# Weight panels of 512 columns by half the rows, for three norms, the queries and the keys

## The chip, the cores and the metric

The kernel runs on one core of a Trainium2 chip. The metric is the device time of one execution, in microseconds (us). The kernel before was run three times: median 2101.73 us, from 2101.66 to 2103.25. A further execution was recorded by the profiler.

## What is computed

Two networks run one after the other over 256 latent tokens `x` and 256 context tokens `ctx` of width 1024, all in float32. The first is two layers of a transformer block. Each layer modulates a normalised input, projects it, and mixes it with two attentions and an MLP:

```python
h_c = modulate(rms_norm(x_ctx, g_attn[l]), csh1, csc1)
h = modulate(rms_norm(x_lat, g_attn[l]), sh1, sc1)
gl, mq, mk, mv, nq, nk, nv = mixer_proj(h, *proj_w)      # h @ w_in, then the low-rank q and kv
...
x_lat = x_lat + gt1 * gated_merge(gl, y_mla, y_na, w_mla_o[l], w_na_o[l], w_out[l])
h2 = modulate(rms_norm(x_lat, g_mlp[l]), sh2, sc2)
x_lat = x_lat + gt2 * squared_relu_mlp(h2, w_ff1[l], w_ff2[l])
```

The context takes the same path in layer 0, and in layer 1 gives only keys and values. The second network starts from this `x_lat` and its own `ctx_2`: an mLSTM layer and then an attention layer whose queries, keys, values and gate are `h @ w_in` of width 2560. Only the latent tokens are returned.

## The kernel before

**Data.** The activations stand transposed in SBUF: `xT` holds 8 chunks of 128 rows for 512 tokens (columns 0 to 255 context, 256 to 511 latent). A norm writes its result as two float32r arrays, `XAh` (rounded) and `XAl` (what rounding left). Weights are treated likewise. They come as **panels** of 1 MB: 8 chunks of 128 rows (`nk`) by 256 columns. The SP queue brings panels in the order of the list that `plan` (line 140) makes, into three `raw` buffers in turn; panel i is fetched when the low half of panel i-3 is made. ACT copies a panel to `whi` (line 1142, `hi`) and DVE subtracts that from the raw panel to give `wlo` (line 1716, `lo`), each in two halves of 1024 columns. There are two `whi`/`wlo` buffers, so the copy of panel i+1 has to wait until PE has used panel i-1 (`p.before`). Of six panels in `POOL_PANELS` (line 117) the low part is made by POOL (line 2366).

**Products.** Each product is three matmuls, high by high, high by low and low by high. `weight_left` (555) has the weights stationary and 512 tokens moving (256 where only latents count): lines 567 to 569. `tokens_left` (594) has 128 tokens stationary and 256 weight columns moving: lines 604 to 606; it makes the na queries and keys, the low-rank queries, the values, and the last queries. It runs through the 8 chunks of one panel for one tile of 128 tokens, with a bank of PSUM for each tile and panel. PSUM banks are taken in turn from six.

**Order.** Each engine's program is written out by hand and runs in that order; they meet at semaphores only. In ACT and DVE a call `begin(p)` makes the split of the panel that follows p. So where ACT or DVE wait, everything behind waits too.

**Norms.** A norm is a sum of squares over the 8 chunks, one matmul with ones on PE (`rms`, 655), a root on ACT (1189) and a reciprocal on DVE (1766), and then chunk by chunk: DVE scales (`scaled`, L1711), ACT writes `XAh` (L1200) and, for odd chunks, the shifted value (L1202), and then DVE (even chunks) or POOL (odd chunks, L2381) writes `XAl`. The context half goes first, the latent half after. PE meets the norm with `weight_pair` (572, lines 588 to 590), and before the last attention layer with its own loop (1060 to 1062): both run over the context half and then the latent half of 8 chunks, and wait before each chunk until its `XAl` is there. `weight_pair` issues 6 matmuls of 256 columns a chunk and half: one panel. The second panel follows as a whole with `weight_left`.

**Three norms** matter here: `n1.0` at the start (at 40 us), `n2.0` ahead of layer 0's MLP (at 492 us), and `s1` ahead of the last attention layer (at 1932 us). Before `n2.0` and `s1` the last residual panel is multiplied by halves while the norm starts (`turn`: 657 on PE, 1204 on ACT, 1791 on DVE).

**The last attention layer** (1043, 1608, 2271) has two panels of keys and values (`atkv`, 256 columns each), four of queries (`atq`, latent tokens only: two tiles), four of the gate (`atz`), then transposes and softmax. ACT takes keys out (L1231), squares them (L1616), DVE sums and normalises them (L2293, L1817, L1702), rotates keys and queries (L1702), and in between makes the low parts of the query panels.

## Time and profile before

| | |
|---|---|
| median of three runs | 2101.73 us |
| the profiled execution, its own time | 2103.66 us |
| its span | 2101.9 us |
| PE busy (matmuls) | 2036.6 us, 97%, 13298 instructions |
| DVE busy | 1133.3 us, 54% |
| ACT busy | 906.8 us, 43% |
| POOL busy | 75.2 us, 4% |
| data moved by DMA | 277.20 MB, mean 132 GB/s |

The profiled execution took 1.8 us longer than its span, which is what lies around the first and last instruction. A matmul's duration in the profile includes a modelled end that overlaps the next one, so "97% busy" doesn't tell how much of the time PE worked at its pace: the distance between the starts of two matmuls does. `LDWEIGHTS` (PEld) overlaps the matmuls.

### The profile page before, as it was taken

Reading aid. Unit: us, or ns where it says so; the run is one execution under the profiler, and the core shown is the slowest. Engines: PE = TensorE matmul, PEld = TensorE weight load, DVE = VectorE, ACT = ScalarE, POOL = GpSimd, SP = SyncE. Lnnn points to the kernel's source line nnn. Section 1 sums busy time; section 2 is a strip of 40 time slices with the busy share of each in tenths; the row PEclk is TensorE's granted clock in tenths of the full one; section 3 lists DMA queues with packets and bytes.
Section 4 is the critical chain, followed back from the end, with each engine's and each line's share of the span. In section 5 each row is a group of like instructions: output and inputs, shape, how many; then the busy total and the mean of one; then the engine's idle time right before and its main releaser. Section 6 shows DMA issues by size and latency. Waiting matters only on the chain. (4 is left out here: it accounts for less than half of the span.)

```text
span 2101.9 us, 32389 instructions
## 1 busy us (share of the span) xinstructions
PE 2036.6 (97%) x13298; PEld 1708.4 (81%) x13298; DVE 1133.3 (54%) x2224; ACT 906.8 (43%) x1648; POOL 75.2 (4%) x89
## 2 busy tenths in 40 slices
PE   5999999999999999999999999999999999999998
PEld 3898767778777777799789899987877777887977
DVE  4447662446433343567665776632555454445876
ACT  4436762325323131355664555433343332234565
POOL 1000000002000000100000000010000000001000
PEclk8999999999999999999999999999999999999999
DMA  7222015533344444433117554444211243222311
GB/s 291 105 77 94 32 42 194 196 132 119 140 182 190 169 161 180 189 134 114 50 63 260 201 185 177 183 165 160 101 61 41 81 180 140 97 85 81 132 50 41
DMA packets 47107, 277.20 MB, mean 132 GB/s; under 512 B 4464, under 2 KB 12784, under 8 KB 16752
## 3 DMA queue, kind: packets, MB, share of 16 engines
q1 hardware_dynamic: 42080, 266.94, 33.7%
q10 hardware_dynamic: 4736, 7.34, 1.0%
q8 instruction: 106, 1.74, 0.3%
q0 software_dynamic: 144, 0.85, 0.1%
q14 instruction: 41, 0.34, 0.0%
HBM read 273.01 MB, written 2.10 MB: 131 GB/s over the span
## 5 line engine op out<-in xcount | busy, mean ns | idle before, releaser
L567 PE MATMUL ps<-t 128*128 128x512 f32 (+1 forms) x2232 | 776.1, 348 | 6.1 <-DVE t L1716 4.6
L568 PE MATMUL ps<-t 128*128 128x512 f32 (+1 forms) x2232 | 768.9, 344 | 0.0
L569 PE MATMUL ps<-t 128*128 128x512 f32 (+1 forms) x2232 | 768.8, 344 | 0.0
L1716 DVE TENSOR_TENSOR t<-t 128x1024 fp32r<-128x1024 f32 (+2 forms) x366 | 410.2, 1162 | 246.0 <-ACT t L1142 245.2
L567 PEld LDWEIGHTS ps<-t 128*128 128x128 f32 x2232 | 421.4, 189 | 72.8 <-issue 9.0
L569 PEld LDWEIGHTS ps<-t 128*128 128x128 f32 x2232 | 421.3, 189 | 52.7
L568 PEld LDWEIGHTS ps<-t 128*128 128x128 f32 x2232 | 421.4, 189 | 51.8 <-issue 0.7
L1142 ACT ACTIVATE t<-t 128x1024 fp32r<-128x1024 f32 (+2 forms) x378 | 359.1, 999 | 189.1 <-PE ps L569 155.4
L1702 DVE TENSOR_TENSOR t<-t 128x512 f32<-128x512 f32 (+10 forms) x621 | 239.6, 405 | 218.7 <-ACT t L1231 78.9
L1231 ACT ACTIVATE t<-ps 128x256 f32<-128x256 f32 (+3 forms) x270 | 121.6, 468 | 402.0 <-PE ps L569 260.5
L604 PE MATMUL ps<-t 128*128 128x256 f32 (+1 forms) x812 | 239.8, 295 | 0.7 <-DVE t L1716 0.5
L606 PE MATMUL ps<-t 128*128 128x256 f32 (+1 forms) x812 | 232.9, 287 | 0.0
L605 PE MATMUL ps<-t 128*128 128x256 f32 (+1 forms) x812 | 232.9, 287 | 0.0
L1711 DVE SCALAR_TENSOR_TENSOR t<-ps,t 128x256 f32<-128x256 f32 (+2 forms) x176 | 83.1, 496 | 179.5 <-PE ps L569 161.8
L604 PEld LDWEIGHTS ps<-t 128*128 128x128 f32 x812 | 155.1, 191 | 9.1 <-issue 3.0
L605 PEld LDWEIGHTS ps<-t 128*128 128x128 f32 x812 | 155.2, 191 | 3.6 <-issue 2.2
L606 PEld LDWEIGHTS ps<-t 128*128 128x128 f32 x812 | 155.1, 191 | 1.4
L1711 DVE SCALAR_TENSOR_TENSOR t<-t 128x256 f32<-128x256 f32 (+6 forms) x226 | 97.5, 457 | 48.5 <-ACT t L1231 34.0
L1702 DVE TENSOR_TENSOR t<-ps,t 128x128 fp32r<-128x128 f32 (+5 forms) x134 | 52.1, 393 | 86.5 <-ACT t L1594 35.2
L634 PE MATMUL ps<-t 128*32 128x256 f32 x1152 | 74.9, 399 | 18.8 <-DMA t<-in_panels 18.1
L1254 ACT ACTIVATE t<-ps,t 128x512 f32<-128x512 f32 (+1 forms) x128 | 87.0, 696 | 10.9 <-DVE t L1702 10.9
L1179 ACT ACTIVATE t<-t 128x256 f32<-128x256 f32 (+1 forms) x62 | 30.9, 503 | 122.8 <-DVE t L1711 106.9
(151 smaller groups left out, 1749.2 us busy)
## 6 DMA issues: line engine op xcount, KB each, us to landing
t<-in_panels SPq DMA_DIRECT2D x236, 1024.0 KB, 4.9
t<-in_panels SPq DMA_DIRECT2D x19, 512.0 KB, 3.8
t<-in_panels SPq DMA_DIRECT2D x6, 768.0 KB, 4.1
t<-in_window ACTq DMA_DIRECT2D x4, 768.0 KB, 4.2
t<-in_ctxT SPq DMA_DIRECT2D x1, 1024.0 KB, 13.3
t<-in_xT SPq DMA_DIRECT2D x1, 1024.0 KB, 15.5
t<-in_ctxT ACTq DMA_DIRECT2D x1, 1024.0 KB, 5.6
t<-in_xT ACTq DMA_DIRECT2D x1, 1024.0 KB, 9.5
```

Source lines behind the costliest of these rows:

```text
L567: e.matmul(o, hi[:, k, w], xh[:, c0:c1], start=k == 0, stop=False)
L568: e.matmul(o, hi[:, k, w], xl[:, c0:c1], start=False, stop=False)
L569: t = e.matmul(o, lo[:, k, w], xh[:, c0:c1], start=False, stop=k == p.nk - 1)
L604: e.matmul(o, xh[:, r], hi[:, k, n0:n1], start=k == 0, stop=False)
L605: e.matmul(o, xh[:, r], lo[:, k, n0:n1], start=False, stop=False)
L606: t = e.matmul(o, xl[:, r], hi[:, k, n0:n1], start=False, stop=k == p.nk - 1)
L1142: e.activation(p.half(whi[p.buf], a), p.half(raw[p.slot], a), ACT.Copy).then_inc(*up(se, ("hi", p.i, a)))
L1231: e.activation(o, i, func, scale=scale).then_inc(*up(se, ("read", key), *names))
L1254: e.activation(work[:, 2 * par + g, x * w:x * w + w], banks(("s", s, i, g))[:, x * w:x * w + w], ACT.Exp, scale=sc_, bias=nm[:, c:c + 1], ...
L1702: e.tensor_tensor(o, a, b, op).then_inc(*up(ve, *names))
L1711: e.scalar_tensor_tensor(o, a, s_, b, o1, o2).then_inc(*up(ve, *names))
L1716: e.tensor_tensor(p.half(wlo[p.buf], a), p.half(raw[p.slot], a), p.half(whi[p.buf], a).bitcast(F32), ALU.subtract).then_inc(*up(ve, ("lo", ...
```

## The change

Eighteen of the panels keep their 1 MB but hold 4 chunks of 128 rows by 512 columns: half the rows and twice the columns. Two such panels replace two of 8 chunks by 256 columns. These are the na queries and keys of both layers (8 panels), the last queries (4), the last keys and values (2), and the first two panels behind each of the norms `n1.0` (`cq`) and `n2.0` (`ff1`) (4). The rest of the list is unchanged. The core of the diff:

```diff
-POOL_PANELS = [("uq", 0, 0), ("ff1", 0, 0), ("ckv", 1, 0), ("uq", 1, 0), ("mq", 0), ("atkv", 0)]
+POOL_PANELS = [("uq", 0, 0), ("ckv", 1, 0), ("uq", 1, 0), ("mq", 0), ("atkv", 0)]
...
+    def halves(key, w, n0, first=0):
+        for a in range(2):
+            panel((*key, first + a), w, 4 * a, 4, n0, 512)
...
+            def weight_four(keys, pair, xs, s, amid=None):
+                o = [bank(key) for key in keys]
+                for x in "cl":
+                    a, b, _ = PARTS[x]
+                    for k in range(8):
+                        p = pair[k // 4]
...
+                        if x == "c" and k % 4 == 0:
+                            weights(p)
+                        rest(p, k % 4)
+                        if amid and x == "c" and k == amid[0]:
+                            amid[1]()
+                        e.wait_ge(*done(("xlo", s, k, x)))
+                        for j in range(4):
+                            w = slice(j * 128, j * 128 + 128)
+                            e.matmul(o[j][:, a:b], hi[:, k % 4, w], xh[:, a:b], start=k == 0, stop=False)
+                            e.matmul(o[j][:, a:b], hi[:, k % 4, w], xl[:, a:b], start=False, stop=False)
+                            t = e.matmul(o[j][:, a:b], lo[:, k % 4, w], xh[:, a:b], start=False, stop=k == 7)
...
+                        if x == "l" and k == 3:
+                            t.then_inc(*up(pe, ("used", p.i)))
+
+            def tokens_half(key, p, xs, tile, last):
+                k0 = p.src[2]
+                o = banks(key) if k0 else bank(key)
...
+                for k in range(4):
+                    xh, xl = xs(k0 + k)
+                    rest(p, k)
+                    e.matmul(o, xh[:, r], hi[:, k, :], start=k0 + k == 0, stop=False)
+                    e.matmul(o, xh[:, r], lo[:, k, :], start=False, stop=False)
+                    t = e.matmul(o, xl[:, r], hi[:, k, :], start=False, stop=k0 + k == 7)
...
                     for tile in tiles if n == "q" else range(4):
-                        tokens_left(("na", l, n, a, tile), p, 0, 256, xa, tile)
+                        tokens_half(("na", l, n, tile), p, xa, tile, tile == 3)
...
                     for k in range(8):
                         shifted(s, k, "c", kind, l, vb)
...
+                        if p2 and k in (3, 5):
+                            hi(p2, (k // 4,))
                         if k == 5:
                             rms(s, "l")
-                    begin(p)
+                    if p2:
+                        nxt[0] = p2.i + 1
+                    else:
+                        begin(p)
...
-                                                       (lambda: last(1, "l"), lambda: stat(s, 7, "l"))])
+                                                       (lambda: last(1, "l"), lambda: stat(s, 7, "l")),
+                                                       *[(lambda a=a: lo(pair, a), lambda: None) for a in range(2) if pair]])
```

`weight_four` (the norms `n1.0` and `n2.0`) issues 12 matmuls of 256 columns a chunk and half, for four chunks of output in four banks, and holds two panels at once: the first is given back after chunk 3 of the latent half, the second at the end. The loop before the last attention layer does the same with tokens stationary: per chunk and half 6 matmuls of 512 columns. `tokens_half` runs 4 chunks of 512 columns for each tile and keeps the tile's bank open until the second panel; results are taken out only then, 512 columns at a time. Columns times matmuls stay the same everywhere; the program has 432 matmuls fewer (528 fewer in the tokens-left products, 96 more where the second panel of `cq` and `ff1` had run with 512 tokens moving).

ACT's and DVE's part: the high and low halves of the second panel of each pair are now made within the context half of the norm, before chunks 4 and 6. In `n1.0` all four halves of the first two panels lie there (before chunks 0, 2, 4 and 6). The low part of `ff1`'s first panel moves from POOL to DVE.

**Place 1: ACT, context half of the norm before the last attention layer.** Names: `t_24` is `xT`, `t_25` is `XAh`, `t_43` is `work`, `t_27` to `t_29` are the raw panels, `t_30` and `t_31` the two `whi`, `t_39` the modulation, `ps_121` PSUM, `t_42` the root. Before, from chunk 2 on:

```order
L1200 ACTIVATE t_25<-t_43,t_39 128x256 x2
L1202 ACTIVATE t_43<-t_43,t_39 128x256
L1179 ACTIVATE t_43<-t_24 128x256
L1200 ACTIVATE t_25<-t_43,t_39 128x256 x2
L1202 ACTIVATE t_43<-t_43,t_39 128x256
L1189 ACTIVATE t_42<-ps_121,t_21 128x256
L1200 ACTIVATE t_25<-t_43,t_39 128x256 x2
L1202 ACTIVATE t_43<-t_43,t_39 128x256
L1142 ACTIVATE t_30<-t_29 128x1024 x2
```

After, from the same point (L1213 is the line that was L1142, L1271 was L1200, L1273 was L1202, L1260 was L1189):

```order
L1271 ACTIVATE t_25<-t_43,t_39 128x256 x2
L1273 ACTIVATE t_43<-t_43,t_39 128x256
L1250 ACTIVATE t_43<-t_24 128x256
L1213 ACTIVATE t_30<-t_29 128x1024
L1271 ACTIVATE t_25<-t_43,t_39 128x256 x2
L1273 ACTIVATE t_43<-t_43,t_39 128x256
L1213 ACTIVATE t_30<-t_29 128x1024
L1260 ACTIVATE t_42<-ps_121,t_21 128x256
L1271 ACTIVATE t_25<-t_43,t_39 128x256 x2
L1273 ACTIVATE t_43<-t_43,t_39 128x256
```

The copy of the second key/value panel came behind the eight context chunks in one piece; now its halves stand before chunk 4 and before the latent half's root.

**Place 2: DVE, start of the norm ahead of the MLP.** `t_32` and `t_33` are the two `wlo`, `t_36` the modulation. Before, from the last whole sum of squares on (L1711 with `ps_121` is a residual):

```order
L1702 TENSOR_TENSOR t_43<-t_43 128x512
L1702 TENSOR_TENSOR t_36<-ps_121,t_19 128x16
L1711 SCALAR_TENSOR_TENSOR t_36<-t_36,t_19 128x16
L1711 SCALAR_TENSOR_TENSOR t_24<-ps_121,t_36,t_24 128x256
L1702 TENSOR_TENSOR t_43<-t_43 128x256
L1711 SCALAR_TENSOR_TENSOR t_24<-ps_121,t_36,t_24 128x256
L1702 TENSOR_TENSOR t_43<-t_43 128x256
L1766 RECIPROCAL t_42<-t_42 128x256
```

After (L1788 was L1716, L1774 was L1702, L1783 was L1711, L1838 was L1766):

```order
L1774 TENSOR_TENSOR t_43<-t_43 128x512
L1788 TENSOR_TENSOR t_33<-t_28,t_31 128x1024 x2
L1774 TENSOR_TENSOR t_36<-ps_121,t_19 128x16
L1783 SCALAR_TENSOR_TENSOR t_36<-t_36,t_19 128x16
L1783 SCALAR_TENSOR_TENSOR t_24<-ps_121,t_36,t_24 128x256
L1774 TENSOR_TENSOR t_43<-t_43 128x256
L1783 SCALAR_TENSOR_TENSOR t_24<-ps_121,t_36,t_24 128x256
L1774 TENSOR_TENSOR t_43<-t_43 128x256
L1838 RECIPROCAL t_42<-t_42 128x256
```

The low part of `ff1`'s first panel, which POOL made, stands on DVE ahead of the residuals of the last two chunks and the reciprocal.

**Place 3: ACT, last attention layer, behind the taking out of the keys.** `t_106` holds the keys, `t_105` the values, `t_110` the keys' sums, `t_102` the queries. Before:

```order
L1616 ACTIVATE t_43<-t_106 128x256 x4
L1142 ACTIVATE t_31<-t_27 128x1024 x2
L1620 ACTIVATE t_110<-t_110 128x16
L1231 ACTIVATE t_105<-ps_121 128x256 x4
L1142 ACTIVATE t_30<-t_28 128x1024 x2
L1231 ACTIVATE t_102<-ps_121 128x256 x2
L1142 ACTIVATE t_31<-t_29 128x1024 x2
```

After, from the last tile on (L1687 takes out keys, L1688 values):

```order
L1687 ACTIVATE t_106<-ps_121 128x256
L1688 ACTIVATE t_105<-ps_121 128x256
L1692 ACTIVATE t_43<-t_106 128x256 x4
L1695 ACTIVATE t_110<-t_110 128x16
L1213 ACTIVATE t_30<-t_28 128x1024 x2
L1213 ACTIVATE t_31<-t_29 128x1024 x2
L1308 ACTIVATE t_102<-ps_121 128x512 x2
```

Before, the copy of a query panel stood between the squares (L1616) and the root (L1620), and another behind the values. Now keys and values are taken out together, and both copies (of the second and third query panel) stand behind the root, which waits for DVE's sums.

## Rows read from the trace of the kernel before

**Rows 1.** Groups by line and shape, PE, whole span: busy, mean ns, idle before.
```profile
L588 PE MATMUL ps<-t 128*128 128x256 f32 x144 | 45.8, 318 | 17.6 <-DVE t L1711 13.3 <-POOL t L2381 4.3
...
L1060 PE MATMUL ps<-t 128*128 128x256 f32 x64 | 19.0, 297 | 5.4 <-DVE t L1711 3.1 <-DVE t L1716 1.3 <-POOL t L2381 1.0
```

**Rows 2.** Page, costliest groups: halves of the weight splits, on DVE and ACT.
```profile
L1716 DVE TENSOR_TENSOR t<-t 128x1024 fp32r<-128x1024 f32 (+2 forms) x366 | 410.2, 1162 | 246.0 <-ACT t L1142 245.2
...
L1142 ACT ACTIVATE t<-t 128x1024 fp32r<-128x1024 f32 (+2 forms) x378 | 359.1, 999 | 189.1 <-PE ps L569 155.4
```

**Rows 3.** Timeline, PE, queries of layer 0: start us, us, engine line op out<-in.
```profile
97.10 0.28 PE L605 MATMUL ps<-t 128*128 128x256 f32 x1
...
99.98 0.28 PE L605 MATMUL ps<-t 128*128 128x256 f32 x1
```

**Rows 4.** Timeline, PE, 512-column matmuls over XAh and XAl.
```profile
90.17 0.39 PE L569 MATMUL ps<-t 128*128 128x512 f32 x1
...
93.57 0.39 PE L569 MATMUL ps<-t 128*128 128x512 f32 x1
```

**Rows 5.** Timeline, PE, tokens-left matmuls of 512 weight columns (ukv).
```profile
175.20 0.40 PE L604 MATMUL ps<-t 128*128 128x512 f32 x1
...
175.90 0.39 PE L604 MATMUL ps<-t 128*128 128x512 f32 x1
```

**Rows 6.** Timeline, PE, first norm: first matmul, clock's rise, third panel's first.
```profile
40.06 0.55 PE L588 MATMUL ps<-t 128*128 128x256 f32 x1 [6.15 <-DVE t L1711]
...
43.27 0.39 PE L588 MATMUL ps<-t 128*128 128x256 f32 x1 [0.31 <-DVE t L1711]
...
67.28 0.39 PE L567 MATMUL ps<-t 128*128 128x512 f32 x1
```

**Rows 7.** Timeline, DVE, same norm, context half.
```profile
38.30 1.23 DVE L1716 TENSOR_TENSOR t<-t 128x1024 fp32r<-128x1024 f32 x1 [3.05 <-ACT t L1142]
...
41.11 1.21 DVE L1716 TENSOR_TENSOR t<-t 128x1024 fp32r<-128x1024 f32 x1
...
45.65 3.16 DVE L1711 SCALAR_TENSOR_TENSOR t<-t 128x256 fp32r<-128x256 f32 x6 [0.18 <-ACT t L1200]
```

**Rows 8.** Timeline, PE, norm ahead of the MLP: first matmul, third panel's first.
```profile
492.16 0.39 PE L588 MATMUL ps<-t 128*128 128x256 f32 x1
...
519.52 0.39 PE L567 MATMUL ps<-t 128*128 128x512 f32 x1
```

**Rows 9.** Timeline, same norm's start on POOL, DVE and ACT.
```profile
480.37 4.93 POOL L2366 TENSOR_TENSOR t<-t 128x1024 fp32r<-128x1024 f32 x2 [343.85 <-ACT t L1142]
...
481.82 1.23 DVE L1702 TENSOR_TENSOR t<-t 128x256 f32<-128x256 f32 x1 [0.54 <-ACT t L1179]
...
484.71 1.28 ACT L1187 ACT_TABLE_LOAD   x1
```

**Rows 10.** Timeline, PE, attention: norm's first, latent half, queries, gate 2.
```profile
1932.42 0.35 PE L1060 MATMUL ps<-t 128*128 128x256 f32 x1 [0.43 <-DVE t L1711]
...
1942.85 0.36 PE L1060 MATMUL ps<-t 128*128 128x256 f32 x1 [1.29 <-DVE t L1711]
...
1962.78 0.28 PE L604 MATMUL ps<-t 128*128 128x256 f32 x1
...
2000.03 0.39 PE L567 MATMUL ps<-t 128*128 128x256 f32 x1
```

**Rows 11.** Timeline, DVE, attention layer, up to the rotation of the queries.
```profile
1955.03 1.39 DVE L2293 TENSOR_REDUCE t<-t 128x4 f32<-128x256 f32 x4
...
1957.83 1.64 DVE L1702 TENSOR_TENSOR t<-t 128x16 f32<-128x16 f32 x5
...
1964.34 2.36 DVE L1716 TENSOR_TENSOR t<-t 128x1024 fp32r<-128x1024 f32 x2 [4.88 <-ACT t L1142]
...
1972.45 2.35 DVE L1716 TENSOR_TENSOR t<-t 128x1024 fp32r<-128x1024 f32 x2
...
1981.62 2.23 DVE L1702 TENSOR_TENSOR t<-t 128x256 f32<-128x256 f32 x6
```

158 lines of the change are left out of this document (93 added, 65 removed).

## The prediction

> **What bounds the kernel now.** I read the groups by line first, then the distance between matmul starts, then the timeline at each stretch that the change touches. PE works almost without a gap, so the time is PE's pace times its matmuls, plus the few places where it waits. The groups name those: line 588 idled 17.6 us before its matmuls over five norms, nearly all of it for `XAl` from DVE (13.3) and POOL (4.3), and line 1060, the last attention layer's norm, 5.4 us [rows 1]. Two of those five norms (`n1.0`, `n2.0`) and the attention's change here. The pace: from 97.10 to 99.98 lie 24 matmuls of 256 columns, 0.120 us each [rows 3]; from 90.17 to 93.57 fifteen of 512 columns, 0.2267 us each [rows 4]. So two narrow ones (0.240) cost 0.0133 us more than one wide one: each matmul carries a fixed part. But wide isn't always that fast: in the `ukv` product, the only one before with tokens stationary and 512 weight columns moving, three take 0.70 us, 0.2333 each [rows 5].
>
> **Term 1, narrow to wide in the na queries and keys.** Layer 0 had 4 tiles x 4 panels x 24 = 384 matmuls, layer 1 2 tiles x 2 panels x 24 + 4 x 2 x 24 = 288. They become half as many: 192 + 144 = 336 pairs. At 0.0133 us a pair: 2.6 us + 1.9 us = **4.5 us**. Bounds: at `ukv`'s pace [rows 5] a pair saves 0.0067, in all 2.2 us; if a wide one took two narrow ones' time, nothing. I take 4.5, since both operands there are `XAh`/`XAl` and `whi`/`wlo`, the same arrays as in rows 4 with their roles changed, while `ukv` has another stationary array. What follows (low-rank queries, rotations, transposes) starts when these products are taken out, so it moves with them. The fewer, wider takings-out lie beside PE.
>
> The Trainium skill ("TensorE: Matmul & The Clock Gate", back-to-back issue gap) gives the gap as N/2.4 + 2.5 ns, so an estimate by it is 109.2 ns and 215.8 ns and a pair would save 2.5 ns, 0.8 us here instead of 4.5. Rows 3 and 4 show 120 and 226.7 ns, and I go by them.
>
> **Term 2, the first norm.** Before, PE ran from its first matmul at 40.06 to the third panel's first at 67.28: 27.2 us [rows 6], for 96 x 0.120 + 48 x 0.2267 = 22.4 us of work. The norm is the reason: a pair of context chunks with half a split in it takes DVE 41.11 - 38.30 = 2.8 us, and a pair without 3.16 / 2 = 1.6 us [rows 7], against PE's 12 x 0.12 = 1.44 us for a pair. After, PE has 24 matmuls for a pair, 2.9 us. All four context pairs now carry half a split (2.8 each, 11.2 in all, against 11.5 of work) and the latent ones none (1.6 against 2.9). PE should run without a stall to the end: 192 x 0.12 = 23.0 us. To this comes the low clock: until 43.27 the matmuls ran at 1.2 GHz (twelve of them in 3.2 us) [rows 6]; now PE has fifteen to put into that time, and 3.2 us at half speed lose some 1.4 us. 24.5 against 27.2: **2.7 us**. Bounds: nothing, if the pairs with a split starve PE, to 3.5. Line 567's 48 wide matmuls have become 96 narrow ones here and in term 3; that costs 48 x 0.0133 = 0.6 us each time and is inside these sums.
>
> **Term 3, the norm ahead of the MLP.** 492.16 to 519.52, 27.4 us [rows 8]. After: 23.0 plus 0.35 for the matmul with ones, plus what follows. DVE now makes the low part of `ff1`'s first panel itself, 2 x 1.16 = 2.3 us [rows 2], ahead of the last two residuals. It is not all late: DVE had waited there for PE's products, and POOL's 4.9 us of work ran beside [rows 9] and is gone. A sum of squares of 256 columns took 1.23 us under it [rows 9], and six like operations later took 2.23, 0.37 each [rows 11]. I get the last sum 0.2 us later and, with the 1.28 us table load behind it on ACT [rows 9], the reciprocal 0.6 us later. PE is busy with modulation rows until 492.1 and doesn't see that, but for 0.2 us. The two halves of the second panel fall into pairs 3 and 4, for which PE has 2.9 us each. So 23.8 against 27.4: **3.6 us**. Behind it, four chunks of output are full at once (two before), at some 2 us each on ACT and DVE: 8 us, and then the next split (2 us and 1.2 us), 11.2 us; PE has 10.9 us in the third panel, but its first outputs are full 1.1 us ahead of the end. It just fits. Bounds 0 and 4.
>
> The Trainium skill ("GPSIMD Engine Reference", specifications and key points) says that GpSimd shares its SBUF interfaces with VectorE, with contention for DVE instructions with two SBUF inputs; the 1.23 us beside POOL and 0.37 us without agree. Without that relief the reciprocal would be some 1.6 us late, and the sum 1 us smaller.
>
> **Term 4, the last attention layer.** PE began the norm at 1932.42, its latent half at 1942.85 after a wait of 1.29 us, and the queries at 1962.78 [rows 10]. Its work in that stretch is 192 narrow matmuls, 23.0 us, of 30.4 us. After: 96 wide ones, 8 chunks x 6 x 0.2267 = 10.9 us a half. The context half is bound by the norm: from 10.4 us it grows by the two halves on DVE, 2.3 us, less about 0.4 of slack, to 12.4. The latent half starts at 1944.85 and ends at 1955.75, **7.0 us earlier**. Not all is kept, since DVE is the next bound. The keys can be squared only when both key and value banks are full and taken out, about 1957.9. DVE's sums then end at 1958.4 instead of 1956.4 (1955.03 + 1.39), and the normalised keys at 1961.5 instead of 1959.5 (1957.83 + 1.64) [rows 11]. Behind it comes the second query panel's low half: ready 1962.7, where PE, after 24 wide matmuls (5.44 us), wants it at 1961.2: 1.5 us of stall. It ends at 1963.85 instead of 1966.70 (1964.34 + 2.36), the rotations of the keys take 5.75 us (to 1972.45) as before, and the third panel's low half is there at 1969.6 + 1.2 = 1970.8, where PE wants it at 1962.8 + 5.4 = 1968.2: another 2.6 us. From there DVE's chain stays 4 us ahead of before, and PE's start of gate 2 moves from 2000.03 [rows 10] to some 1995.9: **4.1 us**. The softmax behind it is unchanged. Bounds: 0, if DVE's chain keeps its old times, and 8.3 (7.0 and 96 pairs of the queries at 0.0133).
>
> **Sum.** 4.5 + 2.7 + 3.6 + 4.1 = 14.9 us. The profiled execution took 2103.66 us (span 2101.9 and 1.8 around it) and would take 2088.8. The median of the runs is 1.9 us below it: 2101.73 - 14.9 = **2086.8 us**. DMA moves the same panels, and each slot is given back earlier or at the same point of the program; I price it at nothing.
>
> **Rivals.**
>
> A. *The wide matmuls aren't faster.* They run at `ukv`'s 0.2333 us, or the fixed part is smaller than rows 3 and 4 say. For it: rows 5 is the only example of this form. Against: another stationary array there. Term 1 falls to 2.2 and term 4 by 0.5 or so: 12.1 us, 2089.6 us; with no gain at all, 2091.9. Chance 0.17. The Trainium skill's gap ("TensorE: Matmul & The Clock Gate", back-to-back issue gap) gives an estimate of 2090.5 us.
>
> B. *The attention layer keeps nothing.* DVE's chain of keys and queries (or the query split behind the root on ACT) is what gate 2 waits for, at its old time. For it: DVE goes from a split at 1964.34 over one at 1972.45 to rotations at 1981.62 [rows 11] with little between. Against: each link that I followed starts earlier. 10.8 us, 2090.9 us. Chance 0.13.
>
> C. *It keeps everything*, because the keys' chain is shorter than I think: 7.0 to 8.3 in term 4, and 4.0 and 3.5 in terms 3 and 2: 20 us, 2081.7 us. Chance 0.09.
>
> D. *Slower: the next split becomes the bound of every wide panel.* A pair holds both `whi` buffers and `tokens_half` needs each panel whole sooner. ACT waits in order for a buffer and for full banks, so if a panel's copy (2.0 us) and low half (1.2 us) can begin only when PE is through with the one before, each of the 12 panels of queries and keys costs up to 3.2 us: 38 us, less 14.9, 2125 us. It decides from 1.6 us a panel (19 us). Against: a token panel is used up as before in four tiles, and its other buffer is free meanwhile; only in layer 1's and the last queries is PE's time for a panel as short as 5.4 us, and it was 5.8 before. Chance 0.03.
>
> E. *Two or three of these partly, nothing left to measure*: within 0.2% (4.2 us, about what a measurement of this kernel can tell from no change). Chance 0.04.
>
> **How the numbers follow.** Forecast 0.54, its own range 2084.5 to 2089. The range to cover 8 in 10 reaches to C on one side (2081.5) and past A and B on the other (2092.5, where terms 1 and 4 both halve and the norms give 5.5); D, E and worse sums lie outside. Faster by over 0.2%: forecast, A, B, C, 0.93. Same 0.04, slower 0.03.
>
> **What would show it.** Wide matmuls over the weights 0.227 us apart in the na stretch (A: 0.233 or more). No gap over 0.3 us in PE between 43 us and the third panel at about 64.5; in the MLP's norm the third panel 23.8 us after the first matmul. In the attention layer a latent half that starts 12.4 us after the context half, queries 23.3 us after it, then two waits of PE for low halves (line 1788 of the changed kernel), of 1.5 and 2.6 us, at the second and third query panel. POOL without its 4.9 us ahead of the MLP. Wrong would be: PE waiting at na panels (D), or gate 2 no closer to the norm's start than the 67.6 us of before (B).

## The result, and the profile after

The changed kernel took 2089.43 us (median of 4 runs, 2088.06 to 2092.04), the kernel before 2101.69 us in the 4 runs beside it (2100.68 to 2103.25). The ratio is 0.9943, its 95% interval 0.9925 to 0.996: 12 us faster, where 14.9 were forecast (2086.8 us; the range of 2081.5 to 2092.5 holds the result, which lies just above the forecast's own range of 2084.5 to 2089). The profiled execution took 2092.04 us, with a span of 2089.3, against 2103.66 and 2101.9 before: 11.6 us by its time, 12.6 by its span. One execution of a kernel further down, the one that takes the gate early, took 3346.17 us at a mean granted clock of 0.56; the ratios leave it out.

Three rows of the groups by shape (line, engine, operation, names, shapes, count | busy us, mean ns | idle us before, by what ended it), changed kernel. They answer to [rows 1]:

```profile
L640 PE MATMUL ps<-t 128*128 128x512 f32 x144 | 57.4, 399 | 3.7 <-DVE t L1788 3.7
L622 PE MATMUL ps<-t 128*128 128x256 f32 x128 | 37.3, 292 | 4.0 <-DVE t L1783 4.0
...
L1128 PE MATMUL ps<-t 128*128 128x512 f32 x32 | 12.9, 403 | 1.0 <-DVE t L1783 1.0
```

Line 588's 17.6 us of idle time came from five norms. The two that changed had 10.8 of them, 8.0 at the first (6.15 of these ahead of its first matmul) and 2.8 at the MLP's. Now line 622 (these two, with four chunks) has 4.0, all ahead of its very first matmul. The three norms that keep the old form, line 598 of the changed kernel, still wait 7.6 us. Line 1060's 5.4 us have become 1.0 in line 1128 (the attention layer's keys and values). What is new is the first row: the wide token products wait 3.7 us, all for line 1788, the low half of a weight panel. PE is busy 97% of the span. The rest of the reading goes by places. Timeline of PE in the changed kernel (start us, busy us, engine, line), the first norm and the na queries:

```profile
41.06 0.55 PE L622 MATMUL ps<-t 128*128 128x256 f32 x1 [4.01 <-DVE t L1783]
...
65.58 0.40 PE L577 MATMUL ps<-t 128*128 128x512 f32 x1
...
94.55 0.47 PE L640 MATMUL ps<-t 128*128 128x512 f32 x1
...
98.76 0.39 PE L640 MATMUL ps<-t 128*128 128x512 f32 x1
...
104.65 0.39 PE L642 MATMUL ps<-t 128*128 128x512 f32 x1
...
289.12 0.50 PE L577 MATMUL ps<-t 128*128 128x512 f32 x1
```

From the first norm's first matmul to its third panel 24.52 us (27.2 in [rows 6]). The wide matmuls over the weights stand 0.2265 us apart (26 of them from 98.76 to 104.65), the pace of [rows 4], not that of [rows 5]. From the first of the na queries (94.55) to the first product behind that layer's attention (289.12): 194.57 us. Then the MLP's norm, where the matmul with ones (line 709) waits for the last residual, and the last attention layer: norm, latent half, queries, second and third query panel, gates, softmax.

```profile
482.15 0.67 PE L709 MATMUL ps<-t 128*128 128x256 f32 x2 [0.86 <-DVE t L1774]
...
488.53 0.39 PE L622 MATMUL ps<-t 128*128 128x256 f32 x1
...
512.08 0.40 PE L577 MATMUL ps<-t 128*128 128x512 f32 x1
...
1922.77 0.47 PE L1128 MATMUL ps<-t 128*128 128x512 f32 x1 [0.44 <-DVE t L1783]
...
1935.74 0.47 PE L1128 MATMUL ps<-t 128*128 128x512 f32 x1 [0.33 <-DVE t L1783]
...
1946.74 0.39 PE L640 MATMUL ps<-t 128*128 128x512 f32 x1
...
1953.71 0.50 PE L640 MATMUL ps<-t 128*128 128x512 f32 x1 [1.37 <-DVE t L1788]
...
1961.81 0.50 PE L640 MATMUL ps<-t 128*128 128x512 f32 x1 [2.32 <-DVE t L1788]
...
1963.09 0.63 PE L641 MATMUL ps<-t 128*128 128x512 f32 x1
1963.52 0.63 PE L642 MATMUL ps<-t 128*128 128x512 f32 x1
...
1988.31 0.39 PE L577 MATMUL ps<-t 128*128 128x256 f32 x1
...
1996.22 0.70 PE L738 MATMUL ps<-t 64*128 64x512 f32 x2
```

The MLP's norm takes 23.55 us (27.4 in [rows 8]). In the attention layer both forecast waits are there, 1.37 and 2.32 us, at the second and third query panel. What follows the second was not forecast: the matmuls start 0.43 us apart, not 0.2267. The window says why (from:to, length, busy us of PE, PEld, DVE, ACT and POOL with the number of instructions, then PEclk, the granted clock as a share of full speed, and at the end the DMA engines' share and GB/s):

```profile
1961.80:1966.00 4.20, 4.19 (x11) 3.31 (x12) 3.71 (x10) 1.62 (x3) 0.00 (x0) 0.59 0.45 138
```

From 1962.5 on PE ran for 3.4 us at 1.2 GHz, and then at 2.4 again (PEclk 1.00 from 1966 on). What the drop costs, and whether it belongs to the wait, the runs have to tell.

Cut at the first matmul of each stage, the 12.5 us between the two first profiles come from these stretches:

| stretch | before | after | difference | forecast |
|---|---|---|---|---|
| start to first norm | 40.06 | 41.06 | +1.0 | 0 |
| first norm to na queries | 56.13 | 53.49 | -2.6 | -2.7 |
| na queries of layer 0 to the end of its attention | 197.04 | 194.57 | -2.5 | -2.6 |
| from there to the MLP's norm | 198.93 | 199.41 | +0.5 | 0.2, inside the next line's |
| MLP's norm to layer 1's na queries | 434.78 | 431.00 | -3.8 | -3.6 |
| layer 1's na queries and attention | 85.01 | 83.47 | -1.5 | -1.9 |
| from there to the last attention layer's norm | 920.47 | 919.77 | -0.7 | 0 |
| that norm to its softmax | 76.32 | 73.45 | -2.9 | -4.1 |
| softmax to the last matmul | 89.53 | 89.54 | 0.0 | 0 |

The 0.7 us in the third line from the end aren't part of the forecast: PE waits there once for a low half before (0.69 us, at 1120.45) and not after. The three kernels below with one of the old parts take 920.4 to 920.6 us for that stretch, the others 919.7 to 920.0 with one exception (next section); why, wasn't followed.

### The profile page after: what moved, and what is told of

The parts are those of the page before. It is cut to its first block and busy times, and to the rows that moved or that the text cites. A ratio compares the mean times of both kernels' runs of the same rounds, so it can differ in the third digit from the quotient of the medians.

```text
span 2089.3 us, 31507 instructions
## 1 busy us (share of the span) xinstructions
PE 2028.2 (97%) x12866; PEld 1684.1 (81%) x12866; DVE 1128.6 (54%) x2226; ACT 905.4 (43%) x1630; POOL 68.2 (3%) x87
## 5 line engine op out<-in xcount | busy, mean ns | idle before, releaser
L577 PE MATMUL ps<-t 128*128 128x512 f32 (+1 forms) x2200 | 763.8, 347 | 6.5 <-DVE t L1788 4.6
L579 PE MATMUL ps<-t 128*128 128x512 f32 (+1 forms) x2200 | 756.4, 344 | 0.0
L578 PE MATMUL ps<-t 128*128 128x512 f32 (+1 forms) x2200 | 756.2, 344 | 0.0
L1788 DVE TENSOR_TENSOR t<-t 128x1024 fp32r<-128x1024 f32 (+2 forms) x368 | 411.9, 1160 | 260.9 <-ACT t L1213 260.1
L577 PEld LDWEIGHTS ps<-t 128*128 128x128 f32 x2200 | 415.4, 189 | 71.8 <-issue 9.4
L579 PEld LDWEIGHTS ps<-t 128*128 128x128 f32 x2200 | 415.3, 189 | 51.4
L578 PEld LDWEIGHTS ps<-t 128*128 128x128 f32 x2200 | 415.5, 189 | 50.7 <-issue 0.7
L1213 ACT ACTIVATE t<-t 128x1024 fp32r<-128x1024 f32 (+2 forms) x378 | 359.5, 999 | 207.1 <-PE ps L579 155.3
L1774 DVE TENSOR_TENSOR t<-t 128x512 f32<-128x512 f32 (+10 forms) x621 | 233.2, 395 | 206.5 <-ACT t L1308 73.2
L1308 ACT ACTIVATE t<-ps 128x512 f32<-128x512 f32 (+1 forms) x244 | 115.9, 493 | 368.5 <-PE ps L579 253.0
L1783 DVE SCALAR_TENSOR_TENSOR t<-ps,t 128x256 f32<-128x256 f32 (+2 forms) x176 | 83.1, 496 | 181.0 <-PE ps L579 160.9
L658 PE MATMUL ps<-t 128*128 128x256 f32 (+1 forms) x524 | 157.9, 301 | 0.4 <-DVE t L1788 0.2
L660 PE MATMUL ps<-t 128*128 128x256 f32 (+1 forms) x524 | 151.4, 289 | 0.0
L659 PE MATMUL ps<-t 128*128 128x256 f32 (+1 forms) x524 | 151.4, 289 | 0.0
L1783 DVE SCALAR_TENSOR_TENSOR t<-t 128x256 f32<-128x256 f32 (+6 forms) x226 | 99.5, 466 | 46.5 <-ACT t L1308 33.9
L658 PEld LDWEIGHTS ps<-t 128*128 128x128 f32 x524 | 99.7, 190 | 8.8 <-issue 3.0
L659 PEld LDWEIGHTS ps<-t 128*128 128x128 f32 x524 | 99.8, 190 | 3.7 <-issue 2.2
L660 PEld LDWEIGHTS ps<-t 128*128 128x128 f32 x524 | 99.7, 190 | 1.4
L1774 DVE TENSOR_TENSOR t<-ps,t 128x128 fp32r<-128x128 f32 (+5 forms) x134 | 52.1, 393 | 88.2 <-ACT t L1667 35.1
```

The lines of the kernel that those rows point to most:

```text
L577: e.matmul(o, hi[:, k, w], xh[:, c0:c1], start=k == 0, stop=False)
L578: e.matmul(o, hi[:, k, w], xl[:, c0:c1], start=False, stop=False)
L579: t = e.matmul(o, lo[:, k, w], xh[:, c0:c1], start=False, stop=k == p.nk - 1)
L658: e.matmul(o, xh[:, r], hi[:, k, n0:n1], start=k == 0, stop=False)
L659: e.matmul(o, xh[:, r], lo[:, k, n0:n1], start=False, stop=False)
L660: t = e.matmul(o, xl[:, r], hi[:, k, n0:n1], start=False, stop=k == p.nk - 1)
```

## The experiments

All kernels below were timed in five rounds against the kernel before on the same chip. Their ratios carry intervals of some 2.5 us to either side, so small differences are read from the stretches of the profiles, which repeat far better: in the profiles of three kernels with the same na stretch it took 194.59, 194.62 and 194.61 us. A difference "by the ratios" is that of two ratios times 2101 us.

### The changed kernel again, twice

Nothing is edited.

> The changed kernel once more, nothing altered: the yardstick for the kernels run beside it, 12 to 14 us under the kernel before. The question is the clock in the last attention layer. In the first profile of the changed kernel PE waited 2.32 us for the low half of the third query panel (line 1788), and the wide matmuls right behind that wait started 0.43 us apart from 1962.7 to 1966.0, at a granted clock of 0.59. If the wait brings the drop, it stands here again, at the same matmuls, and the queries' stretch is some 1.6 us longer than the matmuls and the two waits give. If it was chance in one execution, the matmuls behind the wait start 0.227 us apart here.

> The changed kernel again, as the yardstick for the three kernels run beside it: 12 to 14 us under the kernel before, with PE's two waits for low halves (line 1788) in the last attention layer, 1.4 and 2.3 us, and the low clock behind the second of them if it comes with the wait.

Measured: 2089.12 us, ratio 0.9943 (0.993 to 0.9955), and 2089.48 us, 0.9941 (0.9928 to 0.9953). The stretches repeat, but for four things. The first norm starts at 38.61 and 38.93 us in place of 41.06 (over all profiles of this study it lies between 36.1 and 42.2): the start varies more than most terms of the sum. Layer 1's stretch takes 81.76 and 81.83 us, not 83.47. The low clock behind the third query panel's wait is back in both, for 8 matmuls each. PE's first matmul behind that wait, in the first repetition, and then the window behind it:

```profile
1958.34 0.80 PE L640 MATMUL ps<-t 128*128 128x512 f32 x1 [2.35 <-DVE t L1788]
```

```profile
1958.20:1962.00 3.80, 3.66 (x9) 2.94 (x10) 3.37 (x9) 1.72 (x3) 0.00 (x0) 0.55 0.39 106
```

That matmul takes 0.80 us where the first profile's took 0.50: here the clock was down already when the wait ended. The fourth thing is a low clock with no wait at all. In the second repetition the stretch ahead of the last attention layer takes 921.8 us, and 1.5 of its extra 2 us lie here, in a row of narrow matmuls without an idle time of even 0.1 us in the 27 us before (the granted clock is 1.00 in the four us ahead and in the four behind):

```profile
1507.00:1511.00 4.00, 4.00 (x23) 4.00 (x22) 3.61 (x11) 0.27 (x1) 0.00 (x0) 0.58 0.00 0
```

The first repetition has 35 matmuls in the same window, at 1.00. So PE's clock can also fall where the kernel gives no reason.

### Narrow na panels again

The reading of the weights goes back to `cols(("na", l), w, 0, 8, 3104, 4128)`, and the products with it:

```diff
-                        tokens_half(("na", l, n, tile), p, xa, tile, tile == 3)
+                        tokens_left(("na", l, n, a, tile), p, 0, 256, xa, tile)
```

> The changed kernel with only the na queries and keys put back to matmuls of 256 columns (672 narrow ones in place of 336 wide ones). My theory: each pair of narrow ones costs 2 x 0.120 - 0.2267 = 0.0133 us more than a wide one, and PE is the bound all along: layer 0 2.6 us slower, layer 1 1.9 us slower, 4.5 us in all; the first trace of the changed kernel showed 2.4 and 1.5, so 3.9 at least. Rival A (a wide one saves half as much, or nothing): 2.2 us slower, or no difference. Rival D (the splits bind the wide panels): faster than the changed kernel.

Measured: 2091.05 us, ratio 0.996 (0.9947 to 0.9974), against 0.9943 for the changed kernel beside it: 3.6 us slower by the ratios. PE in this kernel, where the na stretch of layer 0 and that of layer 1 begin and end:

```profile
90.58 0.36 PE L657 MATMUL ps<-t 128*128 128x256 f32 x1
...
287.64 0.50 PE L576 MATMUL ps<-t 128*128 128x512 f32 x1
...
918.13 0.36 PE L657 MATMUL ps<-t 128*128 128x256 f32 x1
...
1001.49 0.68 PE L657 MATMUL ps<-t 128*128 128x256 f32 x1
```

Layer 0: 197.06 us against 194.59 in the changed kernel beside it, 2.47 us, so 2.47 / 192 = 0.0129 us for a pair. Layer 1: 83.36 against 81.76, 1.6 us, 0.0111 for a pair. Together 4.1 us. Rival A (half or nothing) and rival D (the splits bind) are out. Layer 1 also tells how the first two profiles are to be read: 85.01 before and 83.47 after are each some 1.65 us over these, and their difference is the same 1.5. In the changed kernel's first profile the granted clock shows it (0.78 and, in the four us ahead, 0.80, where the repetition has 1.00 at the same places):

```profile
998.20:1002.20 4.00, 4.00 (x27) 3.65 (x26) 2.93 (x7) 2.62 (x7) 0.00 (x0) 0.78 0.11 41
```

### The two norms in their old form

Both four-panel norms go back to two panels ahead and a third behind, and the low half of `ff1`'s first panel to POOL; the main piece of the edit:

```diff
-                        if kind == "cq" and not l and a < 2:
-                            if a == 0:
-                                weight_four([("cq", l, c) for c in range(4)], (p, at["cq", l, 1]), xa, s)
-                            else:
-                                used(p)
-                            wide = False
-                            continue
                         weights(p)
...
-                            weight_pair(keys, p, xa, parts, s)
+                            weight_pair(keys, p, xa, parts, s, None if last else (4, lambda: rms(s, "l")))
```

> The changed kernel with the two norms in four-panel form put back to two panels ahead and a third behind (the latent queries' first panels and ff1's first ones), with POOL's low half of ff1's first panel. My theory: the first norm's stretch to the third panel is 2.7 us longer again (27.2 in place of 24.5), the norm ahead of the MLP 3.8 us (27.4 in place of 23.6), less the 0.5 us by which the reciprocal came later in the changed kernel: 6.0 us slower. Rival: what the norms won is lost again behind them, where four chunks of output are full at once: then 3 us or less, and the third panels of the changed kernel show waits of PE that are not here.

Measured: 2094.09 us, ratio 0.9969 (0.9957 to 0.998), 5.5 us slower than the changed kernel by the ratios. From the first norm to the na queries:

```profile
41.77 0.55 PE L594 MATMUL ps<-t 128*128 128x256 f32 x1 [3.69 <-DVE t L1769]
...
97.91 0.47 PE L636 MATMUL ps<-t 128*128 128x512 f32 x1
```

56.14 us, as before the change (56.13). In the eleven profiles with the four-panel norm and nothing ahead of it that stretch takes 53.49 to 54.59 us, the median is 54.23. So the norm is worth 1.9 us, not the 2.6 of the first pair. The MLP's norm gives 3.9 us back (434.90 to layer 1's na queries against 431.00) and takes 0.45 (198.94 ahead of it against 199.39). 1.9 + 3.9 - 0.45 = 5.4, of 5.5 measured. The rival is out: nothing is lost behind the norms, and PE's third panels show no wait.

### The last attention layer in its old form

`atkv` and `atq` come as narrow panels again, with their loops; of the panels:

```diff
-    halves(("atkv",), w, 1024)
-    for i in range(2):
-        halves(("atq",), w, i * 512, 2 * i)
+    cols(("atkv",), w, 0, 8, 1024, 1536)
+    cols(("atq",), w, 0, 8, 0, 1024)
```

> The changed kernel with only the last attention layer's queries, keys and values (atkv, atq) put back to narrow panels. My theory after the first traces: this part of the change brought 2.4 us (gate 0 and gate 1 of that layer stood 2.3 and 2.1 us nearer to the norm's start), so 2.4 us slower. If the clock drop behind the third query panel's wait was chance and is usually absent, 4 us slower, as in term 4 of the prediction. Rival B (the layer keeps nothing, since DVE's chain of keys and queries is what the gates wait for): no difference.

Measured: 2090.33 us, ratio 0.9954 (0.9941 to 0.9966), 2.3 us slower by the ratios. Its norm and its softmax, and the softmax of the kernel before, whose norm is in [rows 10]:

```profile
1918.99 0.35 PE L1127 MATMUL ps<-t 128*128 128x256 f32 x1 [0.43 <-DVE t L1780]
...
1995.31 0.70 PE L737 MATMUL ps<-t 64*128 64x512 f32 x2 [0.88 <-ACT t L1304]
```

```profile
2008.74 0.70 PE L684 MATMUL ps<-t 64*128 64x512 f32 x2 [0.88 <-ACT t L1231]
```

76.32 us in both, against 73.45, 73.42 and 73.55 in the changed kernel: this part brings 2.9 us. Rival B is out, and so is the sum of 4.1. The expectation of 2.4 was read at gates 0 and 1 and left out what comes behind gate 2: from there to the softmax it is 8.7 us before and 7.9 in the changed kernel (1988.31 to 1996.22), where the first product of the softmax no longer waits 0.88 us for ACT. Why that wait is gone wasn't followed.

### The wait filled with work

Ten wide matmuls that nobody reads go on PE ahead of the third query panel; this is work beside what the reference asks for:

```diff
+                    if a == 2:
+                        o = bank(("filler",), (7,))
+                        for _ in range(10):
+                            t = e.matmul(o, XAh[:, 0, 0:128], XAh[:, 0, :], start=True, stop=True)
+                        t.then_inc(*up(pe, ("read", ("filler",))))
```

> The changed kernel with ten wide matmuls of no use (the tokens by themselves into a free bank, never read) put on PE ahead of the third query panel of the last attention layer, 2.27 us of work where PE waited 2.32 us for that panel's low half. My theory: the low clock behind the wait comes from the idle time; with the filler the wide matmuls of the third panel start 0.227 us apart at once, and this kernel is 1.6 us faster than the changed one, with the same work of use. Rival: the low clock there has nothing to do with the idle time (the power that the chip grants, or chance): the same time as the changed kernel, and the drop is still there or comes and goes in both.

Measured: 2087.73 us, ratio 0.9934 (0.9921 to 0.9946), 1.5 us faster than the changed kernel beside it by the ratios. The filler (line 1141), the third panel behind it, the norm's start and the softmax:

```profile
1921.06 0.47 PE L1128 MATMUL ps<-t 128*128 128x512 f32 x1 [0.44 <-DVE t L1788]
...
1957.59 2.43 PE L1141 MATMUL ps<-t 128*128 128x512 f32 x10
1960.12 0.50 PE L640 MATMUL ps<-t 128*128 128x512 f32 x1
1960.46 0.40 PE L641 MATMUL ps<-t 128*128 128x512 f32 x1
...
1992.98 0.70 PE L738 MATMUL ps<-t 64*128 64x512 f32 x2
```

The third panel starts 39.06 us behind the norm's start, as without the filler (1961.81 - 1922.77 = 39.04), and runs at 0.23 us from the start. The softmax comes 71.92 us behind the norm in place of 73.45: 1.5 us for doing more work. Seven profiles have that wait with nothing in it, and six of them show the drop; in the seventh, the kernel with narrow na panels, it is absent, and there too the softmax comes 71.91 us behind the norm. So the drop costs 1.5 us; it comes with the wait in six of seven profiles, and with the filler in neither of two (the second is below). That speaks for the wait as the cause, though two profiles are few. The 1.5 us by the ratios alone would lie within their intervals.

### A warm-up ahead of the first norm

Twenty matmuls of ones by ones, never read, where PE stands idle ahead of the first norm:

```diff
                 if not l:
                     rows_out()
+                    o = bank(("filler",), (7,))
+                    for _ in range(20):
+                        t = e.matmul(o[:, 0:128], ones[:, :], ones[:, :], start=True, stop=True)
+                    t.then_inc(*up(pe, ("read", ("filler",))))
```

> The changed kernel with twenty matmuls of ones by ones, 128 columns, never read, put on PE ahead of the first norm's first matmul, where PE stands idle for 3.6 to 4.8 us. In seven profiles with the four-panel form the first 13 to 25 matmuls of this norm ran at 1.2 GHz (0.214 us apart in place of 0.120), 2.8 to 5.3 us; with the two-panel form it was 10 matmuls. My theory: the clock rises only after PE has been at work for a while, and the filler's work counts; then fewer than 10 matmuls run at the low clock, the stretch from the norm's first matmul to its third panel takes 23.3 to 24 us in place of 25.0 to 25.6, and the kernel is 1 to 2 us faster. Rival: filler of another type and width doesn't count, or the rise has nothing to do with it: 25 us as before, no difference. A third: the filler delays the norm's first matmul: slower by up to 1 us.

Measured: 2089.46 us, ratio 0.9935 (0.9923 to 0.9947). Windows of PE's clock ahead of and behind the norm's first matmul (38.61 in the changed kernel's repetition, 38.66 with the warm-up), first of the repetition, then of this kernel:

```profile
28.00:32.00 4.00, 2.56 (x26) 1.01 (x20) 2.56 (x2) 1.12 (x3) 0.00 (x0) 1.00 0.97 379
...
36.00:38.50 2.50, 0.00 (x0) 0.00 (x0) 1.66 (x3) 2.50 (x5) 0.42 (x1) 0.61 1.01 400
38.60:40.60 2.00, 1.99 (x9) 2.00 (x10) 2.00 (x3) 1.59 (x5) 0.45 (x1) 0.50 0.39 164
```

```profile
36.00:38.50 2.50, 2.26 (x21) 2.07 (x19) 1.60 (x3) 2.50 (x5) 0.36 (x1) 1.00 1.00 423
```

PE had no matmul from 36.00 to 38.50. The clock had already been at 2.4 GHz when it fell idle, and went down in that gap; the first 20 matmuls of the norm then ran at 1.2 GHz. With work in the gap (the twenty calls stand in the trace as 40 matmuls, 33.63 to 37.99) it stays up, and is 1.00 behind it as well. The stretch to the third panel is 23.55 us in place of 25.19, just the 23.55 of the MLP's norm, so in this one profile all of the first norm's excess over it was the clock. It is 1.6 us by the stretch and 1.3 to 1.7 by the ratios, which is inside their intervals. My reason was half wrong: the filler doesn't bring the clock up, it keeps it from falling.

### Who makes the low half of ff1's first panel

POOL gets it back, ahead of the MLP's norm:

```diff
-POOL_PANELS = [("uq", 0, 0), ("ckv", 1, 0), ("uq", 1, 0), ("mq", 0), ("atkv", 0)]
+POOL_PANELS = [("uq", 0, 0), ("ff1", 0, 0), ("ckv", 1, 0), ("uq", 1, 0), ("mq", 0), ("atkv", 0)]
```

> The changed kernel with the low half of ff1's first panel given back to POOL in layer 0, ahead of the MLP's norm. My theory: DVE loses 2.3 us of work ahead of the last residuals, but POOL's 4.9 us slow its operations beside them (1.23 us for one that took 0.37 elsewhere); PE's longer wait for the reciprocal (0.51 us of growth in the changed kernel) comes down by at most that: 0.5 us faster to 1 us slower, so no difference that can be told. Rival: the time that the MLP norm won comes partly from POOL's absence; then 1 us slower or more, in the stretch from the norm's first matmul to the third panel.

Measured: 2089.37 us, ratio 0.9941 (0.9927 to 0.9955): no difference that the times can tell. POOL's work, one DVE operation behind its start, and the matmul with ones:

```profile
475.28 4.93 POOL L2442 TENSOR_TENSOR t<-t 128x1024 fp32r<-128x1024 f32 x2 [343.59 <-ACT t L1213]
...
479.57 0.92 DVE L1774 TENSOR_TENSOR t<-t 128x256 f32<-128x256 f32 x1 [0.54 <-ACT t L1250]
...
480.64 0.67 PE L709 MATMUL ps<-t 128*128 128x256 f32 x2 [0.36 <-DVE t L1774]
```

The matmul with ones waits 0.36 us for DVE in place of 0.86, the stretch ahead of the norm is 198.90 us again in place of 199.39, and the norm itself takes the same 23.55 us (487.02 to 510.57). POOL does slow the DVE operation beside it (0.92 us; 0.42 at the same place in the changed kernel), yet that is cheaper than 2.3 us more of DVE's own work. The rival is out.

### The query splits earlier, then the gate too

The waits for low halves come from DVE's order, so the order was changed. First the splits alone: `begin` of a panel makes the split of the panel behind it, and these calls moved forward on DVE and ACT. In DVE's program:

```diff
+                begin(at["atq", 0])
                 for tile in range(4):
                     e.wait_ge(*done(("aksq", tile)))
...
+                    if tile == 2:
+                        begin(at["atq", 2])
+                begin(at["atq", 3])
```

> The changed kernel with the splits of the last layer's query panels taken earlier in DVE's and ACT's order (ahead of the key sums, the key rotations and inside the key tiles). My theory: PE's waits at the second and third query panel are there because DVE reaches their low halves late, behind the keys' normalising and rotating; moved ahead, both waits go (1.4 and 2.3 us), and the low clock behind the second with them (1.6 us); the keys come later on DVE, but before gate 0 there are the queries' own sums too, so some comes back: 5 us faster than the changed kernel, some 2084. Rival: the work of DVE is what binds to the gates, and its order changes only where PE waits: the matmuls of the queries run through, and gate 2 starts when it did; within 1 us of the changed kernel. Other rival: the low halves come early but the keys' turn for the gates is late: slower by up to 2 us.

Measured: 2090.64 us, ratio 0.9945 (0.9933 to 0.9958). The queries run through without a wait. The norm's start, gate 0 and gate 1 on PE:

```profile
1921.17 0.47 PE L1128 MATMUL ps<-t 128*128 128x512 f32 x1 [0.44 <-DVE t L1784]
...
1966.90 0.28 PE L577 MATMUL ps<-t 128*128 128x256 f32 x1
...
1980.01 0.55 PE L577 MATMUL ps<-t 128*128 128x256 f32 x1 [5.45 <-DVE t L1775]
```

Gate 0 starts 45.7 us behind the norm (51.7 in the changed kernel), but gate 1 at 58.8 (59.65), after one wait of 5.45 us, and the softmax at 74.5 (73.45). My theory of 5 us is wrong. The first rival has the size, within 1 us, but not the reason: the wait has moved, and a low clock came with it as with the one that it replaced: it fell within the wait, at 1977.7, and lasted to 1984.6, for 21 matmuls. PE waits at gate 1 for DVE to read gate 0's banks, and DVE reads them late:

```profile
1979.43 0.42 DVE L1775 TENSOR_TENSOR t<-ps,t 128x256 f32<-128x256 f32 x1 [0.68 <-ACT t L1721]
```

In DVE's order that operation stands behind the sums of the second half, and it waits for ACT's sigmoid (line 1721), which stands behind that half's root. So the second step takes gate 0 before both.

```diff
+                            gate(0)
+                    if half == 0:
+                        begin(at["atz", 1])
...
-                    if a == 0:
-                        query_root(1)
                     gate(a)
                     if a == 0:
+                        begin(at["atz", 1])
                         for h in range(4):
                             key = ("akT", h)
                             out(key, akT[:, h, :], banks(key), ACT.Copy, "akT")
+                        query_root(1)
```

> The reordered attention layer (its query splits early) with the first gate taken earlier as well: on ACT ahead of the second half's root, on DVE between the first half's rotations. There PE had waited 5.5 us ahead of gate 1, for DVE to read gate 0's bank behind the second half's sums, while DVE itself stood idle some 5 us in three places. My theory: DVE's total work is the bound, and an order that leaves it no idle time brings PE's softmax from 74.5 us behind the norm's start (73.4 in the changed kernel, 71.9 with the filler) to 68 to 70: 3.5 to 5 us faster than the changed kernel, some 2085. Rival: the extra table loads on ACT (1.28 us each, sigmoid, root and sigmoid again) sit in the chain of the second half's root, and the gain is under 2 us. Other rival: the wait only moves once more, and PE waits for the rotated queries of the second half instead: no gain.

> The same reordered kernel with the low half of ff1's first panel back on POOL: my candidate for the fastest. My theory: 0.5 us under the reordered kernel (the stretch ahead of the MLP's norm 198.9 us), so 4 to 5.5 us under the changed one, some 2084.5. Rival: as for the reordered kernel; then no more than 2.5 us under the changed one.

Measured: 2085.87 us, ratio 0.9924 (0.9912 to 0.9937), and with POOL's low half 2085.88 us, 0.9923 (0.9911 to 0.9934): some 4 us under the changed kernel by the ratios, 16 under the one before, the fastest of this study. The second of them:

```profile
1919.63 0.47 PE L1128 MATMUL ps<-t 128*128 128x512 f32 x1 [0.44 <-DVE t L1785]
...
1972.80 0.36 PE L577 MATMUL ps<-t 128*128 128x256 f32 x1
...
1988.19 0.44 PE L1165 MATMUL ps<-t 128*128 128x128 f32 x2 [2.16 <-DVE t L1776]
1989.33 0.84 PE L738 MATMUL ps<-t 64*128 64x512 f32 x2
```

Gate 1 now starts 53.2 us behind the norm, the softmax 69.7 (69.71 and 69.70 in the two kernels), 3.8 us earlier than in the changed kernel: my theory, near its lower end. The table loads on ACT (1.28 us each, at 1970.51, 1976.33 and 1979.18) hold nothing up for long: the middle one ends 1.33 us before the sums that the root waits for. PE's last wait is 2.16 us, among the transposes of the queries. The rotated queries aren't its reason, for DVE is through with them at 1984.88 (first row below). What ends it is DVE's product that reads a bank of gate 2, behind two halves of a split (DVE, same kernel):

```profile
1980.11 4.77 DVE L1776 TENSOR_TENSOR t<-t 128x16 f32<-128x16 f32 x13
...
1985.45 2.35 DVE L1790 TENSOR_TENSOR t<-t 128x1024 fp32r<-128x1024 f32 x2
1987.72 0.75 DVE L1776 TENSOR_TENSOR t<-ps,t 128x256 f32<-128x256 f32 x2
```

So the wait moved once more, to the next bank that DVE gives back late, but only that much of it is left. With that product ahead of the split it should shrink again; that wasn't tried. The second kernel's 0.5 us ahead of the MLP's norm are in its trace (198.94 us), while its softmax met a low clock (from the first matmul of the softmax to the second batch 10.7 us in place of 9.15), so the times don't tell the two apart.

### Filler and POOL together

The edits of two of the kernels above in one.

> The changed kernel with both small gains put together: the ten unused matmuls ahead of the third query panel of the last attention layer, and the low half of ff1's first panel back on POOL. My theory: they are independent. The first took 1.5 us out of the stretch from that norm to the softmax (71.9 us in place of 73.4 to 73.6), the second 0.5 us out of the stretch ahead of the MLP's norm (198.9 in place of 199.4), so 2.0 us faster than the changed kernel, about 2087.2, and no low clock behind the third query panel for the second time. Rival for the clock: its absence with the filler was chance (it was absent once without a filler too, in the kernel with narrow na panels); then it may be back here at 1.2 GHz, with 0.43 us from one wide matmul to the next.

Measured: 2087.96 us, ratio 0.9928 (0.9915 to 0.994), 3 us under the changed kernel by the ratios, 2.0 by the stretches: 71.91 us from norm to softmax and 198.91 ahead of the MLP's norm. No low clock behind the filled wait for the second time:

```profile
1960.29 0.50 PE L640 MATMUL ps<-t 128*128 128x512 f32 x1
1960.63 0.40 PE L641 MATMUL ps<-t 128*128 128x512 f32 x1
```

## Why the prediction was right, and where it was off

The direction, the mechanism and the places were right, and the time lies in the range. The sum of 14.9 us was 2.6 us too large, and no term was too small: the parts measure 1.9 + 4.1 + 3.4 + 2.9 = 12.3 us. That the medians lie 12.3 us apart as well is luck to that digit: the interval of the ratio reaches from 8 to 16 us, and the start and the 0.7 us of the table aren't in the parts.

**Term 1, 4.5 us forecast, 4.1 measured.** The pace of [rows 4] holds with the operands' roles changed, 0.2265 us. That [rows 5] would be the pace was rival A, and the stretches exclude it. The small rest is the size of the saving: a pair costs 0.0129 and 0.0111 us more than a wide one, not 0.0133. The estimate of 0.8 us by the Trainium skill ("TensorE: Matmul & The Clock Gate", back-to-back issue gap), whose formula the page gives for an isolated matmul, doesn't agree with these runs; it is a fifth of the measured 4.1.

**Term 2, 2.7 forecast, 1.9 measured.** The first profile happened to show 24.52 us, the very 24.5 of the forecast; the median of the eleven is 25.29. Two terms were mis-sized. The work was put at 23.0 us, and takes 23.55 at the full clock (the warm-up kernel). And "3.2 us at half speed lose some 1.4 us" took the low clock's length from [rows 6]. In the old form 12 matmuls ran at 1.2 GHz ahead of the first wait for DVE, and the waits hid the rest: the stretch took 56.13 and 56.14 us with the granted clock at 0.77 in the third and fourth microsecond of the norm in one profile and at 0.56 in the other. In the new one PE doesn't wait, so all of it shows: 15 to 27 matmuls start at the low clock, and the stretch lies 1.0 to 2.1 us above 23.55, 1.7 by the median.

**Term 3, 3.6 forecast, 3.4 measured.** The norm's stretch is 23.55 us, with 23.8 forecast, and no wait follows it. The reciprocal came 0.7 us later, as good as the 0.6 forecast (483.52 - 289.12 = 194.40 behind the end of the attention, 486.95 - 293.23 = 193.72 before). The step that failed is "I get the last sum 0.2 us later", and that PE would see but 0.2 us: DVE's last sum ended 0.5 us later (192.88 against 192.36 by the same measure), and PE stood for those 0.5 us at the matmul with ones, which comes before the modulation rows that were to hide the delay. The kernel with POOL's low half back has the old distances and the new norm. What the low half on DVE would cost with POOL still at work beside it ("some 1.6 us late") no run shows. That GpSimd and VectorE contend for SBUF, as the Trainium skill states ("GPSIMD Engine Reference", specifications and key points), does agree with these runs (0.92 us for an operation of 0.42); it just cost nothing here.

**Term 4, 4.1 forecast, 2.9 measured.** Right to 0.7 us were the new length of the context half (12.97 us against 12.4) and the start of the queries behind the norm (23.97 against 23.3), and right were the cause of the two waits and their sizes (1.37 and 2.32 us; as distances between starts 1.5 and 2.5, with 1.5 and 2.6 forecast). Gate 2 stands 65.5 us behind the norm in place of 67.6, where 4.1 us less were forecast. The step that failed is the one behind the waits, "From there DVE's chain stays 4 us ahead". By the prediction's own numbers that chain is 2.85 us ahead (1969.6 against 1972.45); measured from the norm's start it is 2.3 (37.8 against 40.0 us for the third panel's low half). And PE, which would have been some 4 us ahead, lost 1.5 us of that to the clock. Where the drop is absent (the kernel with narrow na panels) gate 2 stands 64.0 us behind the norm, 3.6 us nearer. "The softmax behind it is unchanged" failed too, by 0.8 us the other way. With both the part brings 4.4 us without the drop (76.32 - 71.92): that this is close to 4.1 is partly luck.

Of the rivals, C (everything kept) and D (slower) show nothing of their marks: no wait at an na panel, and waits of PE in the attention layer. B (nothing kept) falls with the kernel in the old form. The start-up, priced at nothing, moved by 1 us in the first pair of profiles and by up to 6 among all. It is no part of the change, and of the 3.5 us between the spans of the changed kernel's first profile and its first repetition it makes 2.45. The traces show part of what starts the first norm late or early: ahead of it PE waits for DMAs of `in_panels`, once for 6.4 to 7.4 us (until 20.5 to 23.1 us) and in some profiles again for up to 2.8 us near 35 us. It wasn't tried.

## What to carry to other kernels

Where PE is busy 97% of the time, halving the number of its matmuls pays just the fixed part of each, and that part is best read as the distance between starts in the kernel's own trace. A shorter PE stage hands the bound to the engine that feeds it: write down that engine's order behind the stage, with durations, as was done here for DVE, and ask of each new wait what the clock does behind it; work of no use in an unavoidable gap can win back what a low clock behind it costs (1.5 us here, for a gap of 2.3). And when a wait is moved by a new order, follow it to where it comes out again before timing: here one step of reordering gave nothing and the next 4 us.

## What the hardware showed that I had not expected

PE's granted clock can fall around a short wait in the middle of dense work. With a wait of 2.32 to 2.37 us it went to 1.2 GHz in six of seven profiles, for 3.4 us. In two of the six it was down when the wait ended, in four it fell 0.5 to 0.9 us later; 7 or 8 wide matmuls started at the low clock, and it cost 1.5 us. In the seventh profile it did not fall. Behind the 1.37 us wait 8 us earlier it never did. Around one of 5.45 us 21 narrow matmuls ran slowly. Behind the last 2.16 us wait of the two fastest kernels it fell in one and not in the other. Filled with matmuls of no use the gap left no trace (two of two). Ahead of the first norm, 20 small products of ones in a gap of 4 us held the clock at 1.00, where it had been 0.61 in the gap and 0.50 behind it.

A wait isn't the only company of a low clock. All fourteen profiles have one at the start of the second network, around waits of up to 2.5 us. Beyond that, one has 3.4 us of it with no idle time before, three have it in layer 1's attention (waits of 0.6 and 0.8 us in the 4 us before, which the others have as well), and seven at the start of layer 1, at the norm of old form, between 885 and 900 us. This last one cost nothing: in the changed kernels the stretch from the MLP's norm to layer 1's na queries takes 430.97 to 431.07 us with it and without it, for there PE waits for DVE and POOL between its matmuls (up to 1.2 us each time). When the clock falls and when it doesn't stays open.
